# First feed-forward of a two-block decoder: four Strassen k pairs in each pair of tiles in place of three, one sum by an accumulating DMA

## Time and profile before

| | |
|---|---|
| median of the runs | 2432.6 us |
| profiled execution: span (the page gives no other time of it) | 2429.9 us |
| TensorE (PE) busy | 2417.6 us, 99% |
| weight loads (PEld) busy | 2008.2 us, 83% |
| VectorE (DVE) busy | 1881.4 us, 77% |
| ScalarE (ACT) busy | 1387.7 us, 57% |
| GpSimd (POOL) busy | 50.6 us, 2% |
| 16 DMA engines, mean rate | 189 GB/s |

### The profile page before, as it was taken

How to read it: one execution, slowest core, us unless ns; L and a number is a source line. 1 busy time by engine, 2 the same in 40 slices (tenths; PEclk the granted TensorE clock), 3 DMA queues, 4 the chain that set the end, 5 groups by cost and what they waited for, 6 DMA issues and landing times.

```text
span 2429.9 us, 29002 instructions
## 1 busy us (share of the span) xinstructions
PE 2417.6 (99%) x11145; PEld 2008.2 (83%) x11145; DVE 1881.4 (77%) x2411; ACT 1387.7 (57%) x1744; POOL 50.6 (2%) x93
## 2 busy tenths in 40 slices
PE   9999999999999999999999999999999999999998
PEld 7888888888888888888888888888788888888887
DVE  6455555688898888989777587664889999999877
ACT  6446555445655555556456464564666666666554
POOL 1000110000000000000001100000000000000000
PEclk9999999999999999999999999999999999999999
DMA  7655555666666666666666555566566666666675
GB/s 238 198 172 155 185 156 162 217 192 191 191 197 200 201 195 203 195 192 202 197 208 198 167 154 161 155 191 197 167 197 193 196 200 188 194 195 189 200 215 169
DMA packets 239299, 460.11 MB, mean 189 GB/s; under 512 B 16582, under 2 KB 18800, under 8 KB 238528
## 3 DMA queue, kind: packets, MB, share of 16 engines
q1 hardware_dynamic: 237760, 452.65, 61.2%
q0 software_dynamic: 1376, 5.69, 0.7%
q10 hardware_dynamic: 32, 0.01, 0.0%
HBM read 456.19 MB, written 2.10 MB: 189 GB/s over the span
## 4 chain that ended last, share of the span: by engine, by line
PE 98%; DVE 1%; DMA 0%; SPq 0%; issue 0%; ACT 0%; DVEq 0%; ACTq 0%
PE acc L1005 16%; PE acc L1007 16%; PE acc L1006 16%; PE acc L721 11%; PE acc L723 11%; PE acc L722 11%; PE mis L1006 3%; PE mis L1005 3%; PE mis L1007 3%; PE mis L694 1%; PE mis L1290 1%; PE mis L819 1%; PE mis L1199 1%; PE acc L740 1%; PE acc L741 1%; PE acc L742 1%
## 5 line engine op out<-in xcount | busy, mean ns | idle before, releaser
L1601 ACT ACTIVATE wf<-wf_raw 128x1024 fp32r<-128x1024 f32 x544 | 568.4, 1058 | 548.3 <-DVE wf_raw L2431 219.1
L2443 DVE TENSOR_TENSOR wf<-wf_raw,wf 128x1024 fp32r<-128x1024 f32 x544 | 643.3, 1219 | 79.1 <-ACT wf L1601 75.6
L2099 DVE TENSOR_TENSOR lo<-raw,hi 128x1024 fp32r<-128x1024 f32 (+1 forms) x313 | 376.5, 1219 | 231.1 <-ACT hi L1354 228.7
L1354 ACT ACTIVATE hi<-raw 128x1024 fp32r<-128x1024 f32 (+1 forms) x313 | 321.0, 1049 | 162.9 <-PE acc L723 139.0
L1005 PE MATMUL acc<-wf,xb_hi 128*128 128x512 f32 x931 | 365.3, 392 | 0.0
L1007 PE MATMUL acc<-wf,xb_lo 128*128 128x512 f32 x931 | 362.7, 390 | 0.0
L1006 PE MATMUL acc<-wf,xb_hi 128*128 128x512 f32 x931 | 362.3, 389 | 0.0
L721 PE MATMUL acc<-hi,xa_hi 128*128 128x512 f32 (+1 forms) x576 | 224.4, 390 | 0.0
L723 PE MATMUL acc<-hi,xa_lo 128*128 128x512 f32 (+1 forms) x576 | 221.8, 385 | 0.0
L722 PE MATMUL acc<-lo,xa_hi 128*128 128x512 f32 (+1 forms) x576 | 221.6, 385 | 0.0
L721 PE MATMUL acc<-hi,xb_hi 128*128 128x512 f32 x544 | 216.4, 398 | 0.0
(11 more groups left out here) (530 smaller groups left out, 3800.0 us busy)
## 6 DMA issues: line engine op xcount, KB each, us to landing
raw<-in_w_in SPq DMA_DIRECT2D x215, 512.0 KB, 4.2
wf_raw<-in_w_ffn_in SPq DMA_DIRECT2D x160, 512.0 KB, 3.7
wf_raw<-in_w_gate SPq DMA_DIRECT2D x88, 512.0 KB, 3.7
wf_raw<-in_w_up SPq DMA_DIRECT2D x88, 512.0 KB, 3.8
wf_raw<-in_w_down SPq DMA_DIRECT2D x88, 512.0 KB, 4.5
wf_raw<-in_w_ffn_out SPq DMA_DIRECT2D x88, 512.0 KB, 4.0
wf_raw<-in_w_out SPq DMA_DIRECT2D x32, 512.0 KB, 4.5
raw<-in_w_o SPq DMA_DIRECT2D x32, 512.0 KB, 4.9
```

What stands on the lines that cost most here:

```text
L1354: nc.scalar.activation(hi[:, slot, :, 0:width], raw[:, slot, :, 0:width], ACT.Copy)\
L1601: nc.scalar.activation(wf[:, f_slot[c], 0, :, :], wf_raw[:, f_slot[c], 1, :, :], ACT.Copy)\
L2099: V.tensor_tensor(lo[:, slot, :, 0:width], raw[:, slot, :, 0:width], hi[:, slot, :, 0:width].bitcast(F32), ALU.subtract).then_inc(lo_ready, 1)
L2443: V.tensor_tensor(wf[:, f_slot[c], 1, :, :], wf_raw[:, f_slot[c], 1, :, :], wf[:, f_slot[c], 0, :, :].bitcast(F32), ALU.subtract).then_inc ...
```

## The change

f1 to f10 get the Strassen k pairs 0, 2, 4 and 5 in place of 0, 3 and 5. The attention's output product (`out`) and the second feed-forward (`ffn2`) keep theirs. The fourth set of token forms for `ffn` is made at the end of f0 and stands where `out` had its first. In f1 to f10 the sum b12 += b22 is no longer VectorE's: GpSimd issues a DMA that adds one 128 x 512 block of SBUF to another in place, once the chunk h = 1 has landed, with two semaphores in turn. VectorE waits for it at the start of the set, makes f2 = b11 + (b12+b22), then f1 = f2 - b22 and f4 = f2 + b21; ScalarE waits for it before it splits the chunk. `gated_up` moves behind the set k = 2.

```diff
-F_S = (0, 3, 5)
+S_K = dict(out=(0, 3, 5), ffn=(0, 2, 4, 5), ffn2=(0, 3, 5))
+S_AT = dict(out=(3, 1, 2), ffn=(0, 3, 1, 2), ffn2=(0, 1, 2))
...
+        adds = [(p, k) for p in ffn_b for k in p.forms]
+        add_g = [p.set(k) for p, k in adds]
+        def t3_made(p, k):
+            g = p.set(k)
+            if g in add_g:
+                j = add_g.index(g)
+                return t3_in[j % 2], 16 * (j // 2 + 1)
+            return t3_ok, g + 1 - sum(x < g for x in add_g)
...
                 if k in p.forms and h == 1:
-                    act.wait_ge(t3_ok, p.set(k) + 1)
+                    act.wait_ge(*t3_made(p, k))
...
                 f_hi_of(p, 3, 0)
+                t_hi_of(p, 2)
                 f_hi_of(p, 3, 1)
                 f_hi_of(p, 4, 0)
-                t_hi_of(p, 3)
                 f_hi_of(p, 4, 1)
                 f_hi_of(p, 5, 0)
+                t_hi_of(p, 4)
...
+                if g in add_g:
+                    dve.wait_ge(*t3_made(p, k))
+                    V.tensor_tensor(f2, b11, b12, ALU.add).then_inc(t2_ok, 1)
+                    yield
+                    dve.wait_ge(t2_ok, g + 1)
+                    V.tensor_tensor(f1, f2, b22, ALU.subtract).then_inc(t1_ok, 1)
+                    V.tensor_tensor(f4, f2, b21, ALU.add).then_inc(t4_ok, 1)
+                    yield
+                    return
...
             x_form_lo("ffn", 2)
+            x_forms("ffn", 3)
             f_lo_of(f0, 7, 0)
             f_lo_of(f0, 7, 1)
+            x_form_lo("ffn", 3)
...
                 f_lo_of(p, 1, 1)
-                f_lo_of(p, 2, 0)
+                strassen(p, 2)
                 gated_up(run_b[p.no - 1])
-                f_lo_of(p, 2, 1)
-                strassen(p, 3)
-                f_lo_of(p, 4, 0)
-                f_lo_of(p, 4, 1)
+                f_lo_of(p, 3, 0)
+                f_lo_of(p, 3, 1)
+                strassen(p, 4)
                 strassen(p, 5)
...
+            for j, (p, k) in enumerate(adds):
+                c = p.chunk(k, 1)
+                slot = f_slot[c]
+                pool.wait_ge(f_in[slot], 16 * f_turn[c])
+                if j >= 2:
+                    pool.wait_ge(t3_in[j % 2], 16 * (j // 2))
+                pool.dma_start(wf_raw[:, slot, 1, 0, :], wf_raw[:, slot, 1, 1, :], accum_op=ALU.add)\
+                    .then_inc(t3_in[j % 2], 16)
```

More of the change, by code:

```diff
@@ L107 @@
 O_S = (3, 5)
-X_ORDERS = ((0, 1, 2), (0, 1, 2), (0, 1, 2))
 E_S = ()
@@ L376, in two_blocks @@
         t1_ok, t2_ok, t3_ok, t4_ok = sem("t1_ok"), sem("t2_ok"), sem("t3_ok"), sem("t4_ok")
+        t3_in = [sem(f"t3_in{j}") for j in range(2)]
         t_hi, t_lo, t_used = sem("t_hi"), sem("t_lo"), sem("t_used")
@@ L499, in two_blocks @@
                 for i in range(first, dict(out=DT // 2, ffn=FT, ffn2=FT, down=DT // 2, down2=DT // 2)[stage]):
-                    nk, forms = KD // CK, F_S
+                    nk, forms = KD // CK, S_K.get(stage)
                     if stage in ("down", "down2"):
@@ L503, in two_blocks @@
                     elif i == first:
-                        forms = dict(out=O_S, ffn=E_S, ffn2=F_S[1:])[stage]
+                        forms = dict(out=O_S, ffn=E_S, ffn2=S_K["ffn2"][1:])[stage]
                     p = Pair(sum(map(len, runs)), run, stage, i, nk, forms, c, g, tile0)
@@ L536, in forms_due @@
         def forms_due(stage, q):
-            at = ("out", "ffn", "ffn2").index(stage)
-            return len(F_S) * at + X_ORDERS[at].index(q) + 1
+            before = ("out", "ffn", "ffn2").index(stage)
+            return sum(len(S_K[s]) for s in ("out", "ffn", "ffn2")[:before]) + q + 1
         def x_place(stage, q):
-            return (xo[:, 0], xo_raw[:, 0]) if stage == "out" and q == 0 else (xf[:, q], xf_raw[:, q])
+            j = S_AT[stage][q]
+            return (xo[:, 0], xo_raw[:, 0]) if j == 3 else (xf[:, j], xf_raw[:, j])
         def sums_of(p):
@@ L1047, in forms @@
                 if p.wide:
-                    return [[x_place(p.stage, F_S.index(k))[0][:, j, f, :] for j in range(2)] for f in range(4)]
+                    return [[x_place(p.stage, S_K[p.stage].index(k))[0][:, j, f, :] for j in range(2)] for f in range(4)]
                 if p.run:
@@ L1072, in strassen @@
                 if p.wide and p.i <= p.run + 1:
-                    pe.wait_ge(xf_lo, forms_due(p.stage, F_S.index(k)))
+                    pe.wait_ge(xf_lo, forms_due(p.stage, S_K[p.stage].index(k)))
                 if p is e1 and k in E_AGAIN:
@@ L1606, in t_hi_of @@
                 tt, tr = t_set(p, k)
+                act.wait_ge(t1_ok, p.set(k) + 1)
                 act.wait_ge(t4_ok, p.set(k) + 1)
@@ L1728, in _ @@
             f_hi_of(f0, 7, 0)
+            x_form_hi("ffn", 3)
             f_hi_of(f0, 7, 1)
@@ L2395, in x_forms @@
             def x_forms(stage, q):
-                k, x, n = F_S[q], xa if stage == "out" else xb, forms_due(stage, q)
+                k, x, n = S_K[stage][q], xa if stage == "out" else xb, forms_due(stage, q)
                 if n > 1:
```

## The result

2553.5 us, the median of four runs (2551.1 to 2558.8), against 2432.7 us beside it: ratio 1.0501, interval 1.0486 to 1.0515. Slower, as forecast, but by 120.8 us and not by 46; the time lies outside the range given.

What follows compares the result with a forecast made beforehand. TensorE was taken to bound, VectorE 4.7 us behind per pair. 9 x 4.5 + 2.2 + 3.5 = +46.2 us, fewer products included, on 2432.6 gave 2478.8 us; range 2445 to 2510.

Steps and rivals of the forecast that it cites:

- Products: In ten pairs, one more Strassen k pair each: 30 fewer matmuls, 6.8 us less.
- VectorE's work in k = 2, and what waits: At k = 2 VectorE idles 4.6 us for the sum, TensorE 2.4 us in k = 2 to 5; again at the turn.
- D: Time of the DMA sum in f1 to f10, from landed chunk to sum in place: 4.2 us, ends 2.6 and 7.6.
- That rival (D of 5.5 to 7.6, chance 0.17): The DMA sum queues behind weight loads: +72 to +114 us, 2505 to 2547 us, chance 0.17.
- 20 D - 37.8: The whole kernel's change in time as a function of D: +46.2 us at the forecast D.
- I cost the slowing of the weight loads at nothing: DMA sums slowing weight loads in ten pairs: priced at nothing; 0.2 us later would add 4 us in all.
- The clock: TensorE's clock expected at 1.00 all through; a lower one behind gaps would add time, with no term given.
- the terms of the sum: Steps of one pair through both waits, k = 2 and k = 0: 46.9 us in place of 42.4, +4.5.
- Turn and k = 7: After the first sums of the next pair's k = 0: turn 0.9 us, then k = 7 with 24 matmuls 5.4.
- The small steps and hand-overs: Within a pair, eight hand-overs between engines and queues at about 0.1 us, taking 46.1 to 46.9 us.
- Seam and end: From f0 to f1 TensorE loses 3.5 us; the last pair, f10, without a second wait, loses 2.2 us.
- The formula 2D + 38.5: Time of a pair in us with D in it twice, in series: 46.9 in place of 42.4.

Runs made afterwards that it cites:

- experiment 1: The changed kernel with all four sums back on VectorE, no accumulating DMA: 2438.8 us, 1.0029 of the kernel before.
- experiment 3: The changed kernel with `middle_end` moved ahead of the wait for the DMA in `to_next`: 2508.5 us, 1.0315 of the kernel before.
- experiment 5: The changed kernel with SyncE holding the load of chunk (3,0) until the in-place sum of k = 2 has landed: 2534.2 us, 1.0421.
- experiment 6: As experiment 5, with the load of chunk (1,0) also held until the sum of k = 0 has landed: 2501.1 us, 1.0282.
- Experiment 4: The changed kernel with 14 matmuls of zeros ahead of the waits at k = 2 and at the turn: 2532.2 us, 1.0407.
- experiment 2: The kernel before with its three k pairs 0, 3, 5, but the sum b12 += b22 by accumulating DMA: 2522.2 us, 1.0366.
- experiment 7: The changed kernel with the accumulating DMA over 256 of 512 columns, the other half of the sum left out: 2527.1 us, 1.0383.
- experiment 11: The changed kernel with the sum as a tensor_tensor on GpSimd itself in place of the DMA: 2446.9 us, 1.0057 of the kernel before.
- experiment 12: As experiment 11, plus `middle_end` moved earlier, f0's third and fourth forms in VectorE's gaps, `gated_up` ahead of set k = 2: 2438.6 us, 1.0025.
- experiment 8: The changed kernel with the DMA sum in k = 5 alone, the other three sums on VectorE: 2450.8 us, 1.0078 of the kernel before.

## Why the prediction was wrong

- **Products: right.** 30 fewer matmuls.
- **VectorE's work in k = 2, and what waits: right in kind.** VectorE does idle at k = 2 and at k = 0, TensorE at k = 2 and at the turn. Experiments 1 and 3 show both.
- **D, the step that failed first.** I took 4.2 us everywhere. Undisturbed it is 3.4, less than my forecast; in the changed kernel it is 6.4 to 6.8 at k = 2 and 4.8 to 5.9 at k = 0 (f2 to f10). I had costed it from rows with no regard to what SyncE issues in the same microsecond, and took the 7.6 us of the one loaded row only as a rival. That rival (D of 5.5 to 7.6, chance 0.17) was right in that loads on the way lengthen the sum, and I gave it too small a chance; with the D measured, 6.0 in the mean of both places, 20 D - 37.8 is +82 us, and the rest of the 120.8 is in the loads and the clock, below. The rows that told it stood in the trace: the order of frees in k = 0 issues two loads 0.7 us apart at 4 us into a pair (774.82 and 775.50 in the trace before), just when the sum of k = 2 goes out. Experiments 5 and 6 show that these neighbours are the cause. In the mean of f2 to f10 the excess is 6.6 + 5.3 - 2 x 4.2 = 3.5 us a pair. By the Trainium skill's page "DMA: Bandwidth & Descriptors" (Anatomy of one DMA — SWDGE) one sum is an estimated 2.6 us; the trace doesn't agree, for even the undisturbed one took 3.4.
- **"I cost the slowing of the weight loads at nothing": wrong.** The load that the sum of k = 0 waits for lands in 4.8 us (issued 789.49, GpSimd's issue 794.31) where 3.7 were taken: 1.1 us in this pair, and 1.3 in the mean of f2 to f10; that of k = 2 adds 0.3.
- **The clock: named and not costed.** I wrote that a lower clock would add to the time, and put 0 in the sum; I also expected it at 1.00 all through, and it was 0.91 in the mean. Experiment 4 shows that it costs time.
- **The pair f3 in the terms of the sum,** all of it from the rows above: the two D are 6.7 + 5.6 = 12.4 us (unrounded) for 8.4, 4.0 more. The two loads are 3.9 + 4.8 for 7.4, 1.3 more. From the sum of k = 2 to the first matmul of k = 5 it is 21.2 us (765.33 to 786.58) for 19.3, 1.9 more, for TensorE is late there at the low clock and no longer waits for VectorE. Turn and k = 7 take 8.0 us (801.29 to 809.33) for 6.3, 1.7 more, again the clock. The small steps and hand-overs are 1.0 less than I had allowed. 46.9 + 4.0 + 1.3 + 1.9 + 1.7 - 1.0 = 54.8, and the pair took 54.8, as did the nine periods in the mean (from the weight loads, (1139.74 - 646.28)/9). So the clock puts an estimated 3.6 us on the path of a pair, where the sum had 0. Filling the gaps took 2.8 us off the mean period of f2 to f9 (52.0 for 54.9) and lost 1.7 in f1; that the other 0.8 is the clock's too was not shown.
- **What I had not seen.** In f4, f5 and f9 TensorE waits at k = 5 too (1.1 to 1.6 us); f4 is the longest pair, 57.8 us.
- **Seam and end.** f1 starts 2.7 us later (646.28 for 643.62), and its k = 0 takes 2.6 more (its weight loads, 7.6 us for 5.0): 5.3 us, where 3.5 were forecast. The nine periods are together 111.8 us longer (493.5 for 381.7), the start 2.7, and what is left of the 121.2 us between the spans, 6.7, falls behind f10's start (2.2 forecast: it too has the 6.7 us sum and the clock).
- **The formula 2D + 38.5** has the two waits right, and doesn't carry far: with D at 3.4 for both (experiment 6) it gives 45.3 us for a pair and a loss of 30 us, where f2 to f9 took 49.2 in the mean and the kernel loses 69. VectorE waits a third time there, 0.9 to 2.4 us at k = 4 from f2 on, the held loads may be late for other chunks, and the clock is still 0.98. These were not separated.

Open: whether the sum waits for the loads' packets in the DMA engines or at the memory; no run tells these apart.

## What to carry to other kernels

An operation moved to a DMA takes work off an engine and is paid for with latency, and the latency counts where an engine in order waits for it, with everything behind it in its list; lay the sum's issue beside the issues of the loads on a time line before pricing it, since neighbours doubled it here. Count waits that stand in series through a ring of slots, and give each gap of several us on TensorE a price for the clock behind it too. An idle engine's own instruction (1.5 us on GpSimd) beat its DMA (3.4 to 6.8 us) by 107 us. The order of a list counts too: moving `middle_end` alone took back 45 us.

## What the runs showed of the hardware

- An accumulating DMA from SBUF to SBUF of 128 x 512 float32 takes 3.4 us from GpSimd's issue to VectorE's start when no load is issued beside it (experiments 5 and 6), 4.5 to 6.1 with one load of 512 KB issued within 0.6 us of it, 6.4 to 6.8 with two within 0.7 us. In experiment 2 it takes 5.2 to 5.8 us with two loads issued 1.1 to 3.0 us ahead of it and none beside it, so loads that are already on the way count too. Its issue takes GpSimd 0.86 us, where plain loads took it 0.48 to 0.78 in the trace before (the landing times of some are in the earlier trace rows).
- With half the columns (experiment 7): 2.7 to 2.8 us to ScalarE's start at k = 4 in five of the six pairs whose next load is issued 1.3 us or more behind it, and 5.5 to 6.0 to VectorE's beside two loads.
- VectorE's operations get longer where GpSimd adds beside them, by 0.06 us in the mean of a low part (experiment 11) and 0.52 us for `gated_up` (experiment 12).
- With two gaps of some 4 us a pair the granted clock was 0.91 in the mean from 640 to 1050 us; it was 1.00 in experiments 1, 4 and 8, where TensorE's longest waits from f2 on are 0.5, 1.6 and 1.4 us.
